# Hybrid encoder trunk, RWKV part: a second transposition on the Vector engine for the inverses, the state update on ACT, keys and bonus in another place

## What is computed

```python
def step(state, inp):
    r_t, w_t, k_t, v_t, kk_t, a_t = inp
    sa = jnp.einsum('bhvk,bhk->bhv', state, -kk_t)
    state = (state * w_t[:, :, None, :]
             + sa[..., None] * (kk_t * a_t)[:, :, None, :]
             + v_t[..., None] * k_t[:, :, None, :])
    y = jnp.einsum('bhvk,bhk->bhv', state, r_t)
    return state, y
...
k_bonus = 0.5 * (k_f + k_b)
bonus = jnp.sum(heads(r * k_bonus) * r_k, axis=-1, keepdims=True) * heads(v)
```

## Time and profile before

| quantity | value |
|---|---|
| median of 3 runs | 1866.26 us (1866.06 to 1869.93) |
| the profiled execution, device time | 1867.6 us |
| its span (first to last instruction) | 1865.7 us |
| mean granted TensorE clock, of full | 0.939 |
| PE busy | 1652.5 us, 89% |
| DVE busy | 1007.7 us, 54% |
| ACT busy | 732.9 us, 39% |
| RWKV rounds of layer 0, start of the first to end of the last | about 280 to 507 us |
| RWKV rounds of layer 1 | about 1194 to 1412 us |

### The profile page before, as it was taken

The page is one execution under the profiler, slowest core; times in us unless marked ns, Lnnn a source line. Parts: engine busy times, 40 slices in busy tenths (PEclk is TensorE's granted clock), DMA queues, the critical chain, the costliest instruction groups (busy, mean ns, idle before and its releaser), DMA issues.

```text
span 1865.7 us, 28024 instructions
## 1 busy us (share of the span) xinstructions
PE 1652.5 (89%) x11272; PEld 1213.6 (65%) x11272; DVE 1007.7 (54%) x1533; ACT 732.9 (39%) x1201; POOL 289.4 (16%) x124
## 2 busy tenths in 40 slices
PE   2997866888998999989989978588889899999997
PEld 0784433666676888877757834266667688887885
DVE  6644558778217667754443244588752454445333
ACT  3434234665624232222233343456654422223223
POOL 1342000000032222211224400000002122222121
PEclk8998996989999999999989989789889999999999
DMA  7344110000043554443303210000002222222221
GB/s 294 135 161 158 47 75 1 2 2 2 2 147 118 198 191 180 180 158 135 129 9 124 91 68 1 0 2 2 2 2 91 68 90 90 97 105 90 77 103 68
DMA packets 34653, 163.00 MB, mean 87 GB/s; under 512 B 3840, under 2 KB 4096, under 8 KB 25856
## 3 DMA queue, kind: packets, MB, share of 16 engines
q1 hardware_dynamic: 34560, 161.65, 24.7%
HBM read 159.54 MB, written 2.10 MB: 87 GB/s over the span
## 4 chain that ended last, share of the span: by engine, by line
PE 57%; issue 26%; DVE 8%; ACT 4%; POOL 3%; DMA 1%; POOLq 0%; SPq 0%; DVEq 0%; ACTq 0%
PE bank L500 8%; PE bank L502 8%; PE bank L501 8%; PE bank_pair L500 3%; PE bank_pair L502 3%; PE bank_pair L501 3%; PE bank L547 2%; POOL work_parts L1925 2%; PE bank_pair L603 2%; PE bank L840 2%; PE bank L841 2%; PE bank L818 1%; PE bank L656 1%; POOL proj_weights_parts L1920 1%; PE bank L516 1%
## 5 line engine op out<-in xcount | busy, mean ns | idle before, releaser
L500 PE MATMUL bank<-work_parts,y_mix_parts 128*128 128x512 f32 x792 | 316.2, 399 | 21.4 <-DVE work_parts L1689 10.3
L502 PE MATMUL bank<-work_parts 128*128 128x512 f32 x792 | 315.3, 398 | 0.0
L1702 DVE TENSOR_TENSOR work_parts<-work,y_mix_parts 128x1024 fp32r<-128x1024 f32 x66 | 169.7, 2570 | 254.9 <-ACT y_mix_parts L970 254.9
L1920 POOL TENSOR_TENSOR proj_weights_parts<-proj_weights,proj_weights_hi_parts 128x1024 fp32r<-128x1024 f32 x54 | 130.1, 2416 | 934.1 <-ACT proj_weights_hi_parts L966 857.8
L1925 POOL TENSOR_TENSOR work_parts<-work,y_mix_parts 128x1024 fp32r<-128x1024 f32 x66 | 159.1, 2411 | 609.8 <-ACT y_mix_parts L970 609.8
L970 ACT ACTIVATE y_mix_parts<-work 128x1024 fp32r<-128x1024 f32 x132 | 133.0, 1054 | 261.1 <-DMA work<-mlp_dram 251.3
L501 PE MATMUL bank<-work_parts,y_mix_parts 128*128 128x512 f32 x528 | 208.4, 395 | 0.0
L500 PEld LDWEIGHTS bank<-work_parts,y_mix_parts 128*128 128x128 f32 x792 | 150.9, 190 | 59.1 <-issue 24.7
L502 PEld LDWEIGHTS bank<-work_parts 128*128 128x128 f32 x792 | 150.5, 190 | 35.8
L500 PE MATMUL bank<-work_parts,proj_weights_hi_parts 128*128 128x512 f32 x272 | 112.1, 412 | 26.2 <-DVE work_parts L1689 24.5
L501 PEld LDWEIGHTS bank<-work_parts,y_mix_parts 128*128 128x128 f32 x528 | 99.9, 189 | 24.1
(11 more groups left out here) (266 smaller groups left out, 3056.6 us busy)
## 6 DMA issues: line engine op xcount, KB each, us to landing
work<-mlp_dram SPq DMA_DIRECT2D x66, 1024.0 KB, 4.8
work<-ada_dram SPq DMA_DIRECT2D x64, 512.0 KB, 4.6
proj_weights<-tiles_dram SPq DMA_DIRECT2D x57, 512.0 KB, 3.6
x_res<-ada_dram SPq DMA_DIRECT2D x24, 512.0 KB, 4.9
x_res<-x_dram SPq DMA_DIRECT2D x2, 2048.0 KB, 10.6
mixer_inputs<-ada_dram SPq DMA_DIRECT2D x8, 512.0 KB, 17.8
work<-mlaw_dram SPq DMA_DIRECT2D x4, 640.0 KB, 4.5
out_dram<-x_res SPq DMA_DIRECT2D x8, 256.0 KB, 2.2
```

Of the source, the lines that this page charges most:

```text
L500: mm(out, w_hi, x_hi, start=start, stop=False)
L502: return mm(out, w_lo, x_hi, start=False, stop=stop)
L1702: TTT(MW_L[q][:, 1], MW_IN[q][:, 1], plain(MW_H[q][:, 1]), ALU.subtract).then_inc(msp_v.sem, msp_v.one("l1"))
L1920: pool.tensor_tensor(ring_l[s], ring[s], plain(ring_h[s]), ALU.subtract).then_inc(spl_q.sem, spl_q.one(f"t{s}"))
```

## The change

Four things change, all in the RWKV rounds.

1. **The level.** X0T, which held the 32 transposed blocks, is now written by a second DVE stream transposition ("trans", 32 partitions x 1024), placed after "join" and ahead of the old one ("out"). The 32 PE transpositions (L561) and the two ACT copies (L1081) go. The mask of Gram matrix 0 moves between the two transpositions. PE waits for "trans" before its first multiplication and for "out" before its second. On ACT the copies of the first product now come ahead of the two diagonal copies.
2. **The state update.** It moves from DVE (one multiplication, 128x128) to ACT (`scan_next`: two scaled copies of 128x64, one per direction, with the decay as a per-partition scale), behind the `scan_solve` copies of the same step and ahead of all other work of the step.
3. **Keys and bonus** of block cur + 2 are computed on DVE at the end of round cur, behind the mask of Gram matrix 1, and no longer in steps 0 and 1 of round cur + 1.
4. **Order on PE and ACT.** Triangle direction 0 of the block after next stands behind the second level product instead of between the two, its copies behind the last copies of the level. Triangle direction 1 stands behind `scan_update` of step 0 instead of ahead of it. `tail_centre` moves from the end of step 0 into step 1, between `scan_state` and `scan_solve`.

The diff, without the tables of semaphore steps and most unchanged lines:

```diff
@@ -555,14 +556,7 @@
...
                         keep_clock(it, stage, count)
-                pe.wait_ge(inv_v.sem, inv_v.at("out", it))
-                for d in D2:
-                    for m in range(16 * d, 16 * d + 16):
-                        last = pe.transpose(PS[1 + d][0:32, (m % 16) * 32:(m % 16) * 32 + 32], XD[0:32, m, :], ident[0:32, 0:32])
-                    own(lev_p, last, f"X{d}")
-                scan_gram(it, 1)
-                scan_values(it, 0)
-                pe.wait_ge(lev_a.sem, lev_a.at("X1", it))
+                pe.wait_ge(inv_v.sem, inv_v.at("trans", it))
                 for i in range(16):
@@ -570,8 +564,9 @@
...
                             own(lev_p, ins, f"T{d}")
-                if early:
-                    rwkv_triangle(it + 1, 0)
+                scan_gram(it, 1)
+                scan_values(it, 0)
+                pe.wait_ge(inv_v.sem, inv_v.at("out", it))
                 pe.wait_ge(lev_a.sem, lev_a.at("T1", it))
@@ -581,6 +576,8 @@
...
                                 own(lev_p, ins, f"Z{e}")
+                if early:
+                    rwkv_triangle(it + 1, 0)
                 scan_tokens(it, b, 1)
@@ -634,7 +631,7 @@
...
                 cur = SM[s % 2]
-                pe.wait_ge(sc_v.sem, sc_v.at(f"S{s - 1}", it))
+                pe.wait_ge(sc_a.sem, sc_a.at(f"S{s - 1}", it))
                 for d, e in pairs:
@@ -697,22 +694,22 @@
...
                             scan_state(it, s)
+                        if trail and s == 1:
+                            if build:
+                                pe.wait_ge(tri_a.sem, tri_a.at("B10", new))
+                            tail_centre(old)
                         scan_solve(it, s)
...
                             scan_values(it, s + 1)
+                        last = scan_update(it, s)
                         if s == 0 and build:
                             rwkv_triangle(new, 1)
-                        last = scan_update(it, s)
                         if s == 0:
...
                             scan_tokens(it, cur, s + 2)
-                    if trail and s == 0:
-                        if build:
-                            pe.wait_ge(tri_a.sem, tri_a.at("B10", new))
-                        tail_centre(old)
                     if trail and s == 2:
@@ -1077,20 +1074,18 @@
...
                 for d in D2:
-                    act.wait_ge(lev_p.sem, lev_p.at(f"X{d}", it))
-                    own(lev_a, F(X0T[0:32, 16 * d:16 * d + 16, :], sixteen(PS[1 + d][0:32, :]), ACT.Identity), f"X{d}")
+                    act.wait_ge(lev_p.sem, lev_p.at(f"T{d}", it))
+                    own(lev_a, F(X0T[32:64, 16 * d:16 * d + 16, :], sixteen(PS[1 + d][64 * d + 32:64 * d + 64, :]), ACT.Identity), f"T{d}")
+                act.wait_ge(inv_v.sem, inv_v.at("out", it))
                 for q in range(2):
                     diagonal(it, q)
-                for d in D2:
-                    act.wait_ge(lev_p.sem, lev_p.at(f"T{d}", it))
-                    own(lev_a, F(X0T[32:64, 16 * d:16 * d + 16, :], sixteen(PS[1 + d][64 * d + 32:64 * d + 64, :]), ACT.Identity), f"T{d}")
                 scan_state(it, 0)
-                if early:
-                    triangle(it + 1, 0)
                 for e in range(2):
...
                     own(lev_a, F(XT[it % 2][rows, :, :, 32:64], PS[1 + e][rows, :].rearrange("p (d c t) -> p d c t", d=2, c=NCH), ACT.Identity), f"Z{e}")
+                if early:
+                    triangle(it + 1, 0)
@@ -1109,6 +1104,15 @@
...
                 own(sc_a, last, f"SA{s}")
+
+            def scan_next(it, s):
+
+                if s == 0:
+                    act.wait_ge(pre_v.sem, pre_v.at("em1", it))
+                act.wait_ge(sc_p.sem, sc_p.at(f"S{s}", it))
+                for d in D2:
+                    last = F(SM[(s + 1) % 2][:, d, :], PS[1][:, 2 * P + d * C:2 * P + d * C + C], ACT.Identity, scale=EM[it % 2][:, d, s:s + 1])
+                own(sc_a, last, f"S{s}")
@@ -1148,6 +1152,8 @@
...
                         scan_solve(it, s)
+                        if s < NCH - 1:
+                            scan_next(it, s)
                     if scan and s == 0:
@@ -1582,6 +1588,8 @@
...
                 settle(dve, "dve")
+                own(inv_v, dve.transpose(X0T[0:32].rearrange("p m t -> p t m"), XL[0:32, 0:1024].rearrange("p (c i) -> p c i", c=32)), "trans")
+                scan_ring(it, 0)
                 own(inv_v, dve.transpose(XD[0:64].rearrange("p m t -> p t m"), XL[0:64, 0:1024].rearrange("p (c i) -> p i c", c=32)), "out")
@@ -1595,12 +1603,6 @@
...
                     f"G{s}")
-
-            def scan_state(it, s):
-
-                dve.wait_ge(sc_p.sem, sc_p.at(f"S{s}", it))
-                own(sc_v, TTT(SM[(s + 1) % 2], PS[1][:, 2 * P:3 * P].rearrange("p (d v) -> p d v", d=2),
-                              EM[it % 2][:, :, s].unsqueeze(2).to_broadcast([P, 2, C]), ALU.mult), f"S{s}")
@@ -1622,21 +1624,13 @@
...
                 for s in range(NCH):
-                    if scan and s < NCH - 1:
-                        scan_state(it, s)
                     if scan and s < NCH - 2:
...
                         if s == 0:
-                            if scan:
-                                keys(new, nxt, 0)
                             inverse_in(new)
                             inverse_half(new)
-                            if scan:
-                                keys(new, nxt, 1)
                         if s == 1:
-                            if scan:
-                                bonus(new, nxt)
                             inverse_8(new, 1, 5)
@@ -1669,7 +1663,6 @@
...
                 if build:
-                    scan_ring(new, 0)
                     if early:
@@ -1681,6 +1674,10 @@
...
                     scan_ring(new, 1)
+                    if early:
+                        for d in D2:
+                            keys(new + 1, nxt + 1, d)
+                        bonus(new + 1, nxt + 1)
```

11 lines of the change are left out of this document (6 added, 5 removed).

## The result

| | before | changed |
| --- | --- | --- |
| median of 20 runs | 1866.3 us | 1873.2 us |
| lowest to highest | 1860.4 to 1874.1 | 1866.3 to 1883.9 |
| ratio to before, 95% interval | 1 | 1.0043 (1.0030 to 1.0056) |
| profiled execution, its span | 1865.7 | 1872.0 |

The change is slower by 8 us by the ratio (5.6 to 10.5), and by 6.8 us by the medians. The forecast was 6.6 us faster, and 1873.2 lies above the upper end of its range, 1869.

The account below looks back on a forecast made before the run. PE, ACT and DVE were taken to bound the RWKV rounds in turn (edge, step, side work). Layer 0's -5.5 and layer 1's -1.1 us made -6.6, so 1866.3 would become 1859.7 us; range 1851 to 1869, the forecast's own 1855 to 1863.

Parts of the forecast that it names:

- The edge: Stretch from the end of the useless matmuls to a round's first solve; forecast 5.2 us for 7.1 to 7.4.
- DVE's chain: DVE's work from join to the end of the transposition into lanes; summed to 18.2 us, 18.4 before, the new limit.
- step 1: Second scan step, trail rounds: 2.91 us of ACT side work before the next right-hand side; round 2 of layer 0: -0.25.
- Part 1: The level: solve 0 2.1 us earlier, 1.9 where the edge takes 7.1, about 1.4 at half clock; most doesn't get through.
- Part 2: The update on ACT: 0.56 us for 0.29, hidden by 0.1 in a plain step, but ACT's other work starts later.
- The dearer effect is the queue: ACT's other work starts about 1.25 us later behind the update; 0.8 us without loss, 1.75 beside a large matmul.
- the list: Step-by-step effects of ACT's later queue against before, for steps 1, 4, 5, 6 and round 3; entries from -0.8 to +1.9 us.
- Step 5: `early_decay` on ACT, 1.15 us, with a table load of 1.28 in round 1: +0.45 in round 0, +1.25 in round 1.
- step 4 of round 2: `inverse_second` on ACT, 1.71 us, without the saved bonus wait that rounds 0 and 1 have: +0.9 us.
- The second rival: PE reaches `scan_state` before ACT's update is done, some 0.2 to 0.3 us on roughly 40 steps: 1869 us, chance 0.14.
- The first rival: More gets through: if half clock leaves four edges, each gives 1.5 to 2 us more; 1852 us, chance 0.16.
- The third rival: No difference, 1866 us: DVE binds step 1 and round 0's gain shrinks, or queue losses are twice as large; chance 0.20.

Follow-up runs that it names:

- mask_first: no_update with mask 1 put ahead of the queries and removals of direction 1 on DVE; ratio to before 0.9927.
- no_update: The changed kernel with the state update back on DVE, all else as changed; 1861.8 us, ratio to before 0.9962.
- the fill: The changed kernel with six useless matmuls ahead of each solve where PE waits (step 2 of rounds 1 to 3, step 6 of round 1); 1866.1 us, ratio 1.0001.
- only_update: The kernel before with the state update moved to ACT and nothing else; 1896.8 us, ratio to before 1.0143.

## Why the prediction was wrong

**Right.** The useless matmuls hide both transpositions (first product straight behind them). The transposition took 1.94 to 1.95 us for 1.96. The edge takes 5.26 us for 5.2 in round 3, where it has no triangle. The update's pair takes 0.52 us for 0.56 and is hidden in plain steps (3.49 and 4.35 us, as before). DVE's chain from the end of the join to the end of the transposition into lanes is 17.9 us (414.79 to 432.72), for 18.2 summed; but it wasn't what step 1 waited for. The early product waits no longer, step 4 to 5 is 4.57 for 5.39 us. Round 0 gained 5.3 us a layer for a forecast of 4.8, in part by luck: its solve 2 came 15.0 us after the edge began and not 13.9, solve 6 to 7 took 0.8 us more than before, and from solve 7 to the next join it gained 1.6 us where the sum had 0.7.

**Part 1, mis-sized.** "1.9 where the edge takes 7.1" holds in round 3 and in one other edge. In rounds 0 to 2 the edges took 6.7 us on average in two profiles each, for 7.7 before: a gain of 1.1 us (in the changed kernel's first profile 6.7, 6.1, 6.8 and 6.7, 7.4, 5.3). I had priced half clock in one edge, and nine of these twelve had it for 0.9 to 4.1 us (before, four of twelve); in another PE sat idle for 1.12 us amid the triangle for a reason that the profile doesn't show. And of DVE's one transposition more I wrote only what it does behind mask 2, not who waits for the removals (0.68 us) and for mask 1 (2.10 us behind the first solve of round 1, layer 0). That wait is in the order of both kernels: Gram matrix 2 waits for mask 1. mask_first (6.5 us less, intervals that overlap slightly) suggests that it is on the path. The transposition moved every DVE instruction behind it by about 2 us, and I had looked for the last one alone.

**Part 2, the step that failed.** "The dearer effect is the queue" was right, and its price was the failure: the list sums to about 4 us for the program with step 1 at -0.25, and part 2 measured 15 us. In that list, step 1 was right as a length: 5.42 us from solve 1 to solve 2 in the run, 2.35 + 2.91 + 0.37, or 5.6, by my working. The error was to set it off against an edge that would be 2.1 us shorter. Step 5 was right in round 1 (5.07 for 3.85, +1.2 for +1.25), step 4 of round 2 too (+0.7 for +0.9). Solve 6 to 7 was priced only for round 2's `tail_scale`, +0.5, and cost 0.7 us there, 0.8 in round 0, and 1.3 to 1.6 us in round 1, where PE was at half clock. Of the 12.5 us by which the rounds of the changed kernel, mean of its two profiles, are longer than those of no_update, solve 1 to 2 makes 6.8, solve 5 to 6 2.9, solve 6 to 7 6.2 and solve 2 to 3 1.6; 1.6 us between solves 4 and 5 and 5.0 between solve 7 and the join go off, and the rest lies ahead of solve 1. Round 3 lost 1.4 us, where I set 1.9 against 1.9.

The larger part of the gap, 8 us by the fill, is a term that the sum didn't have: what PE's idle does to its clock. I wrote of the clock only for the edge and its useless matmuls. With the update on ACT and no filler the rounds have 61 to 89 us at half clock, with it on DVE 31 to 58, and as the table shows, PE's matmuls alone take 7 to 15 us longer in the changed kernel than in no_update. The fill gave 8 us back with no wait removed. Part 2 costs 15 us in the changed kernel and 27 us alone, about half by waits and half by clock where it is alone (11 us of idle, 10 to 14 of busy time).

**Rivals.** The second rival's figure of 1869 is the nearest, but its mechanism isn't what happened: matmuls waited for the update itself for 1.5 us in the whole program. Its rule pointed the right way, though not for the reason that the rule gives. The Trainium skill ("ScalarE: Activation LUTs", section "Rules for kernel authors") puts multiplications on VectorE for its speed per element. The pricing that the prediction took from the same page stands in its section "What ACT_TABLE_LOAD costs"; it gave 0.57 us for the pair and the trace 0.52. So the loss isn't in the instruction's price but in the queue behind it. The first rival (more gets through, 1852) isn't borne out either: level and keys without part 2 came to 1856, but with half clock still in five of their six edges with a triangle. Without part 2 the changed kernel is 7 us faster than before by its ratio, where my sum without part 2's 4 us would give 10.6: some 3.5 us of the miss are the gain of the other parts, summed too large, and some 11 us the loss of part 2, summed too small. The third rival had the right places in its second half, queue losses twice as large as taken, but not the clock, and 1866 for the 1873 measured; the range ended at 1869 because no case in it priced idle in slower matmuls.

What stays open: why level and order are worth such different amounts beside each other, and where 6 of the 8 us lie, which the two pairs of profiles don't show in the rounds. The sizes of 3 to 7 us rest on intervals that meet or overlap, and the profiles scatter by as much.

## What to carry to other kernels

When an instruction is moved to another engine, price what stands behind it in that engine's queue at every step, and not only whether its own result is in time: here the result was in time and the move cost 15 to 27 us. When one engine's queue gets longer, list every consumer of every instruction behind the insertion, the early ones above all (mask and removals, not only the end of the chain). Nor is the old place free: on DVE, behind keys and bonus, the same update made PE wait 1.6 us. And where TensorE is the bound, count a microsecond of new idle on it as up to two, since matmuls behind it may run at half clock (in only_update 11 us of idle came with 10 to 14 us of slower matmuls).

## What the hardware showed

Useless matmuls placed in waits of 1.4 to 1.9 us made the program 8 us faster (1.0043 to 1.0001), with 48 of them added. One idle of 1.86 us was followed by half clock in one profile of the kernel and by full clock in another; two such steps make 3.1 us of the 4.9 between its rounds of 371.4 and 376.3 us. Over twelve profiles of like kernels, each us at half clock went with 0.43 us more of PE's busy time. The part of the program with unchanged code took 1488.5 to 1500.6 us in 20 profiles. A pair of scaled copies of 128x64 from PSUM took 0.52 us on ACT, 0.31 us each, where DVE needs 0.29 for both halves in one instruction. A stream transposition of 32x1024 on DVE took 1.93 to 1.98 us and one of 64x1024 2.01 to 2.09.
